# Gathered token columns packed to 104 a pass instead of 128, in a two-layer decoder step with routed experts

## The reference

```python
scores = jax.nn.sigmoid(x @ router_w)                  # 320 tokens x 64 experts
_, eidx = lax.top_k(jnp.where(emask, sel, -jnp.inf), 8)  # 8 experts a token
w = take(scores, eidx); w = w / sum(w) * 2.5
# for each expert e, over the tokens that chose it:
hb = jax.nn.silu(xb @ wg[e]) * (xb @ wu[e])            # 1024 -> 256
y[tok] += (hb @ wd[e]) * w[:, None]                    # 256 -> 1024
```

## Time and profile before

| | |
|---|---|
| median of 3 runs | 1434.81 us (1434.44 to 1436.46) |
| the profiled execution | 1434.92 us, its span in the trace 1433.1 us |
| TensorE (PE) busy | 1395.9 us, 97% |
| VectorE (DVE) busy | 437.7 us, 31% |
| ScalarE (ACT) busy | 317.1 us, 22% |
| expert loop of layer 0 | 247.5 to 705.7 us |
| expert loop of layer 1 | 954.5 to 1412.6 us |
| loads by SyncE's queue | 489.96 MB of 509.52 MB |

### The profile page before, as it was taken

How to read it: one execution, slowest core, us unless ns; L and a number is a source line. 1 busy time by engine, 2 the same in 40 slices (tenths; PEclk the granted TensorE clock), 3 DMA queues, 4 the chain that set the end, 5 groups by cost and what they waited for, 6 DMA issues and landing times.

```text
span 1433.1 us, 20787 instructions
## 1 busy us (share of the span) xinstructions
PE 1395.9 (97%) x8288; PEld 706.4 (49%) x8288; DVE 437.7 (31%) x1161; ACT 317.1 (22%) x746; POOL 48.1 (3%) x86
## 2 busy tenths in 40 slices
PE   7999999999999999999999999999999999999997
PEld 3345657444445444444465456564444444444443
DVE  1146535312221222122345243442121312122214
ACT  2134323111111111111345113411111111111113
POOL 0100302000000000000100010010000000000000
PEclk9999999999999999999999999999999999999998
DMA  9999528999999999999972245389999999999993
GB/s 393 389 381 427 214 103 311 392 390 427 421 423 426 421 425 425 424 426 424 422 320 118 118 162 219 112 336 380 425 424 423 426 423 421 425 424 426 425 424 126
DMA packets 48002, 509.52 MB, mean 356 GB/s; under 512 B 5808, under 2 KB 6208, under 8 KB 8320
## 3 DMA queue, kind: packets, MB, share of 16 engines
q1 hardware_dynamic: 44144, 489.96, 82.1%
q0 software_dynamic: 3760, 18.20, 3.4%
HBM read 499.10 MB, written 11.01 MB: 356 GB/s over the span
## 4 chain that ended last, share of the span: by engine, by line
PE 88%; DMA 4%; DVE 3%; ACT 3%; issue 1%; SPq 0%; DVEq 0%; ACTq 0%
PE bank L2044 26%; PE banks L2094 13%; PE banks L1946 10%; PE banks L442 5%; PE ybank L1974 3%; PE banks L1119 3%; PE banks L1974 3%; PE bank L1976 3%; DMA s_gu_ring<-in_moe_up_dram 3%; PE bank L504 2%; PE ybank L1738 1%; PE banks L1738 1%; DMA s_gu_ring<-in_ada_w_dram 1%; PE banks L697 1%; PE banks L1124 1%; PE banks L671 1%
## 5 line engine op out<-in xcount | busy, mean ns | idle before, releaser
L2044 PE MATMUL bank<-s_gu_ring,s_hbuf 128*32 128x512 f32 (+1 forms) x2688 | 395.2, 593 | 1.4 <-DVE s_hbuf L2169 0.9
L2044 PEld LDWEIGHTS bank<-s_gu_ring,s_hbuf 128*32 128x32 f32 (+1 forms) x2688 | 121.9, 119 | 265.9 <-issue 265.9
L2094 PE MATMUL banks<-s_dn_ring,s_hTs 128*32 128x512 f32 (+1 forms) x1344 | 204.2, 596 | 0.0
L2214 DVE TENSOR_TENSOR s_ylo<-banks,s_yhi 128x512 fp32r<-128x512 f32 x112 | 77.5, 692 | 320.2 <-ACT s_yhi L2136 320.2
L1946 PE MATMUL banks<-s_sel,s_htok 128*128 128x512 f32 (+1 forms) x640 | 144.8, 374 | 0.5 <-issue 0.5
L1946 PEld LDWEIGHTS banks<-s_sel,s_htok 128*128 128x128 f32 x640 | 106.2, 188 | 60.7 <-issue 44.3
L2136 ACT CAST s_yhi<-banks 128x512 fp32r<-128x512 f32 x112 | 65.7, 586 | 296.5 <-PE banks L2094 296.5
L2209 DVE SCALAR_TENSOR_TENSOR s_hh<-s_sg,s_wsl,bank 128x256 f32<-128x256 f32 x56 | 26.9, 480 | 288.1 <-ACT s_sg L2127 288.1
L2094 PEld LDWEIGHTS banks<-s_dn_ring,s_hTs 128*32 128x32 f32 (+1 forms) x1344 | 55.9, 118 | 118.0 <-issue 117.3
L2127 ACT ACTIVATE s_sg<-bank 128x256 f32<-128x256 f32 x56 | 21.6, 385 | 364.8 <-PE bank L2044 364.8
L2169 DVE COPY s_hbuf<-banks 128x512 f32<-128x512 f32 (+1 forms) x60 | 39.4, 656 | 96.0 <-PE banks L1946 96.0
(11 more groups left out here) (463 smaller groups left out, 1452.5 us busy)
## 6 DMA issues: line engine op xcount, KB each, us to landing
s_gu_ring<-in_moe_up_dram SPq DMA_DIRECT2D x128, 2048.0 KB, 15.2
s_dn_ring<-in_moe_wd_dram SPq DMA_DIRECT2D x128, 1024.0 KB, 12.8
s_gu_ring<-in_ada_w_dram SPq DMA_DIRECT2D x24, 2048.0 KB, 13.0
s_gu_ring<-in_win_dram SPq DMA_DIRECT2D x6, 2048.0 KB, 12.8
s_gu_ring<-in_wqkv_dram SPq DMA_DIRECT2D x6, 1024.0 KB, 19.4
s_gu_ring<-in_wo_dram SPq DMA_DIRECT2D x2, 2048.0 KB, 18.8
s_gu_ring<-in_shared_up_dram SPq DMA_DIRECT2D x2, 2048.0 KB, 9.8
s_gu_ring<-in_gwo_dram SPq DMA_DIRECT2D x2, 2048.0 KB, 10.8
```

What stands on the lines that cost most here:

```text
L2044: last = pe.matmul(W0[o:o + n, :], tokens_of(p, k)[:, o:o + n], w[:, k, :, :], start=(k == 0), stop=(k == KC - 1))
L2094: last = pe.matmul((W1, W2)[half][o:o + n, :], hTs[:, f, o:o + n], dn_ring[:, DN_PLACE[dn_of[(l, r)][0]], w0:w0 + 512], start=(f == 0), st ...
L2214: dve.tensor_tensor(ylo[:, half, :], (W1, W2)[half], yhi[:, half, :].bitcast(F32), ALU.subtract).then_inc(S["y_low"], 1)
```

## The change

Each rank gets a number of gathered columns of its own (`ROOMS`, at most its capacity), and a pass has `PITCH[q]` gathered columns: 104, and 112 in batch 1. `gathered` gives each rank's first column. The rows of the pass, its capacities and the weight loads' sizes stay as they are. So:

- `select` writes one instruction for each rank, with as many columns as its room; fills move 416 columns (448 in batch 1, 208 in batches 0 and 7).
- The gate and up products still take 32, 64 or 96 rows for a rank, from its packed first column on; beyond its room they read the next rank's tokens.
- `spread` takes the place of `dense`: it clears `selb` and copies each rank's columns to its row places, so rows beyond a room have weight zero.
- At the start of a layer's loop VectorE clears columns 104 to 127 of every block of `hbuf`, after it has waited for fill 1.
- `pass_plan` pairs the fullest ranks with the emptiest: (2, 63), (3, 62) and so on, and among the 64-row ranks the first with the last.
- `sg` and `hTs` move into the router's memory, and `selb` gets its own.

```diff
+ROOMS = (
+    (52, 52, 96, 93, 92, 85, 82, 82, 80, 76, 63, 62, 60, 60, 58, 57, 56, 55, 54, 54, 52, 52,
...
+PITCH = (104, 112, 104, 104, 104, 104, 104, 104)
...
-    wide = [[(NFIX + i, 96), (NE - n96 + i, 32)] for i in range(n96)]
-    middle = [[(r, 64), (r + 1, 64)] for r in range(first64, first32 - light, 2)]
+    wide = [[(NFIX + i, 96), (NE - 1 - i, 32)] for i in range(n96)]
+    middle = [[(first64 + i, 64), (last64 - 1 - i, 64)] for i in range((last64 - first64) // 2)]
...
+def gathered(l, experts):
+    out, at = [], 0
+    for r, cap, o in places(experts):
+        out.append((r, ROOMS[l][r], o, at))
+        at += ROOMS[l][r]
+    return out
...
-                        width = P * BATCHES[q]
+                        width = PITCH[q] * BATCHES[q]
...
-                                last = pe.matmul(W0[o:o + n, :], tokens_of(p, k)[:, o:o + n], w[:, k, :, :],
+                                last = pe.matmul(W0[o:o + n, :], tokens_of(p, k)[:, o - back_by[r]:o - back_by[r] + n], w[:, k, :, :],
...
+                        w = PITCH[q]
                         for h in range(BATCHES[q]):
+                            for r, n, _, at in gathered(l, PASSES[l][BATCH_START[q] + h]):
+                                last = dve.tensor_tensor(sel[:, :, h * w + at:h * w + at + n],
...
-                    def dense(q):
-                        n = P * BATCHES[q]
-                        for t, (t0, tn) in enumerate(TILES):
-                            last = dve.tensor_copy(selb[t][0:tn, 0:n], sel[0:tn, t, 0:n].bitcast(F32))
+                    def spread(q):
+                        step(dve.memset(selb[:, :, 0:P * BATCHES[q]], 0.0))
+                        w = PITCH[q]
+                        for h in range(BATCHES[q]):
+                            for r, n, o, at in gathered(l, PASSES[l][BATCH_START[q] + h]):
+                                last = dve.tensor_copy(selb[:, :, h * P + o:h * P + o + n], sel[:, :, h * w + at:h * w + at + n].bitcast(F32))
...
+                    dve.wait_ge(S["fill_full"], filled(0, 1))
+                    dve.memset(hbuf[:, :].rearrange("p (x s) -> p x s", s=P)[:, :, PITCH[0]:P], 0.0)
                     fill_out(0, 1)
                     fill_out(0, 3)
```

More of the change, by code:

```diff
@@ L151, in const_table @@
     put("keyrow", np.broadcast_to(NE - 1 - np.arange(NE) + ahead, (P, NE)))
-    for name, plan in zip(("caprow", "caprow1"), PASSES):
-        cap = np.zeros(NE)
-        for r, slots in sum(plan, []):
-            cap[r] = slots
-        put(name, np.broadcast_to(cap, (P, NE)))
+    for name, room in zip(("caprow", "caprow1"), ROOMS):
+        put(name, np.broadcast_to(np.array(room), (P, NE)))
     half = HD // 2
@@ L1955, in slot_weights @@
                             for s, (t0, tn) in enumerate(TILES):
-                                last = pe.matmul(W0[:, at:at + n6].rearrange("p (e u) -> p e u", u=6), selb[s][0:tn, P * j:P * j + P],
+                                last = pe.matmul(W0[:, at:at + n6].rearrange("p (e u) -> p e u", u=6), selb[0:tn, s, P * j:P * j + P],
                                                  wpartS[0:tn, s, :, ranks[0]:ranks[-1] + 1:ranks[1] - ranks[0]].rearrange("p u e -> p e u"), start=(s == 0), stop=(s == 2))
@@ L2179, in _ @@
                     dve.wait_ge(S["sel_full"], l * NB + 1)
-                    dense(0).then_inc(S["w_parts"], 1)
+                    spread(0).then_inc(S["w_parts"], 1)
                     dve.wait_ge(S["sh_silu"], 2 * l + 2)
@@ L2199, in _ @@
                     step(select(1))
-                    dense(1).then_inc(S["sel_full"], 1)
+                    spread(1).then_inc(S["sel_full"], 1)
                     dve.wait_ge(S["wall_full"], l * NB + 1)
@@ L2222, in _ @@
                             step(select(q + 2))
-                            dense(q + 2).then_inc(S["sel_full"], 1)
+                            spread(q + 2).then_inc(S["sel_full"], 1)
                     rest_dve(dve, left)
```

49 lines of the change are left out of this document (21 added, 28 removed), and 5 rows, old and new, of the table ROOMS.

## The result

The changed kernel takes 1438.45 us (median of 12 runs, 1437.48 to 1441.66), the kernel before in the same series 1435.16 us (12 runs, 1434.44 to 1436.67). The ratio is 1.0021, with a 95% interval of 1.0014 to 1.0029: slower by 3.3 us by the medians and by 3.0 us by the ratio. The prediction set 0.2% as the bound between "within" and "slower", and the interval reaches to both sides of it. The forecast was 1435.3 us with a range of 1430.5 to 1439.5, and "within 0.2%" had the most of the three chances (0.57; slower had 0.20). The profiled execution took 1437.77 us (before 1434.92), its span is 1436.0 us (before 1433.1).

A forecast was written before the change was run, and what follows sets the result against it. The prediction took the load queue as the bound, 0.35 us longer than TensorE's chain. From 1434.92 us it took 3.4 for earlier loads and added 3.8 for the low clock: 1435.3 us, range 1430.5 to 1439.5.

The forecast's parts named there:

- What bounds the kernel: Expert loops: the load queue outlasts TensorE's work by 0.35 us, so TensorE's saved 11.2 us a layer mostly becomes load waits.
- The rival with TensorE as the bound: Whole run: the queue can exceed 426 GB/s, so all 22.4 us saved on TensorE arrive; 1412.5 us, chance 0.03.
- The clock: Pass 27 of each layer: the wait ahead drops TensorE to half rate, losing 1.9 us a layer, 3.8 us in both.
- a start that it called a hint: Kernel start: matmuls reached full pace after 4.3 us, about 3.7 us of it work; gave the 1.9 us loss.
- the clock holds: Rival, last passes: the clock stays full through the waits, so only the queue's gain counts; 1431.5 us, chance 0.18.
- The long low clock: Rival, pass 27: half rate through all gate and up products costs 7.1 us a layer; 1445.7 us, chance 0.08.
- The start of the loop: First pass of a layer: starts 0.2 us earlier, with bounds from 0.6 us earlier to 0.6 us later.
- The load queue: Each layer's last load lands 1.7 us earlier, 1.3 us from the loads behind pass 2; 3.4 us in both layers.
- small gaps: Later loop slices at 420 to 424 GB/s instead of 426: closing them gives the load queue 0.4 us a layer.
- `spread` and `hh`: `spread` ends about 253.3, 1 us before needed: no wait; `hh` may show 0.1 to 0.2 us in four passes.
- VectorE's chain at the start: Rival: first pass starts 0.6 us late and is held up 0.8 us, cancelling the queue's gain; 1438.7 us, chance 0.12.
- The change does what it says: Rival: a rank exceeds its room, so `rest` reloads 64 experts, 201 MB or 473 us; 1908 us, chance 0.01.

The follow-up runs named there:

- light kernels: Kernel before and changed kernel, each loading only half of every expert's down weights, used twice: 4250.14 and 4231.72 us; only layer 0's loop is comparable.
- awake2: Changed kernel plus 11 and 22 extra small matmuls on TensorE ahead of the load waits of passes 26 and 27: 1434.95 us, ratio 1.0000.
- pool: Changed kernel with the clearing of `hbuf`'s columns moved from VectorE to GpSimd: 1439.32 us, ratio 1.0026 to the kernel before.
- hold_awake: awake2 with each layer's last three down loads issued only once its last gate/up load has landed: 1440.49 us, ratio 1.0041.
- hold_best: Changed kernel, shared down products moved as in shift_after, 7 and 22 extra matmuls, last three down loads held as in hold_awake: 1434.00 us, ratio 0.9990.
- shift_after: Changed kernel with the shared expert's down products for tokens 0 to 127 moved from pass 1's end to behind pass 2's gate/up products: 1436.15 us.
- wide: Changed kernel with rooms equal to capacities and pitch 128 again, nothing cleared in `hbuf`, new pairing and `spread` kept: 1435.19 us, ratio 1.0000.
- light_before: Kernel before, loading only the first half of each expert's down weights and using it twice, which changes layer 1's routing: 4250.14 us.

## Why the prediction was right in kind, and what it mis-sized

**What bounds the kernel.** Right. TensorE's saving became waits for loads at the places and of the lengths forecast (5.80 for 5.9 us; 3.06 for some 3 us), and the light kernels show that the saving is real (9.9 us a layer from pass 0 on; the prediction's 11.2 contained 1.7 us for 208 columns, and its own caveat was more than half right: 1.21 for 1.29 us a ten, 0.7 us in all). The rival with TensorE as the bound is out.

**The clock.** Right that it falls and costs time at pass 27, and near in size. In layer 0 it fell in the wait as forecast; in layer 1 only 0.8 us after the wait had ended. It cost 8.40 - 7.07 = 1.33 us in layer 0 and 8.77 - 7.07 = 1.70 us in layer 1. Together 3.0 us in the profile and 3.0 to 3.5 us in the runs (awake2 against the changed kernel), for which the prediction had 3.8. What was left of the low clock when layer 0's load had landed was 2.7 us (691.32 to 694.05), and half of that is the 1.33 us lost. In layer 1 all of it lay in the pass (1400.61 to 1404.02). The forecast took its price from a start that it called a hint, so that it is this near is in part luck. The rival "the clock holds" is out by awake2. The long low clock, through all the gate and up products, is out by the stretch 694 to 696, at 0.99, in the first half of pass 27. The Trainium skill, "TensorE: Matmul & The Clock Gate", section "What's actually happening", has idle time bring the low clock back. The fall at 690 to 692 agrees; the one at 1400.61 came when TensorE was at work again. Pass 26 of layer 0, at 7.07 us after a wait of 3.06, shows that a wait of that length doesn't always do it.

**The start of the loop.** Mis-sized. Forecast: 0.2 us earlier. Measured: pass 0 starts 6.29 us behind the first fill for 5.93, 0.36 us later in both layers. The step that failed is the fill of 208 columns. Ten were to take 1.08 us; the first 30 took 3.57, 1.19 a ten. The first fill also began 0.08 us later. The second fill had ended at 243.95 instead of 243.7, and VectorE's memset began at 244.41 instead of 243.9, so some 0.2 us of its delay came between the two and has no cause shown; the memset itself (0.70 us) was as forecast. The measured value was inside the bounds of -0.6 to +0.6 that were given. pool moves this term and the time does not follow, so it matters only through the next one.

**The load queue.** This is the term that failed: 1.7 us a layer forecast, 3.4 us in both. In the profile pass 27 starts 0.56 us earlier in layer 0 and 0.34 us *later* in layer 1. In the runs awake2, which has the narrow columns and no low clock, stands at 1.0000 of the kernel before, with an interval of 1.3 us to both sides. Its first step was right: from pass 0 to the loads behind pass 2 are 292.94 - 247.95 = 44.99 us instead of 46.10, which is the 1.1 us of two passes' fills. With the later start 0.75 us remain in layer 0 (0.65 in layer 1), where 1.3 was forecast: 1.2 us of the missing 3.2 us for both layers. The 0.4 us a layer of small gaps came as forecast: from 100 to 446.4 us behind the first fill the queue moved 0.2 MB more than before, 0.5 us.

What failed besides is the step from the whole queue to one load, "so the last load of a layer lands 1.7 us earlier". I added up the queue's packets in the traces, from the issue of a layer's first expert load, 55.6 us ahead of its first fill. At 446.4 us behind the first fill the changed kernel had moved 195.10 MB in layer 0 and 195.06 in layer 1, the kernel before 194.62 in both: at 425 GB/s the queue was 1.1 and 1.0 us ahead. But when the last gate and up load landed, 196.38 and 196.66 MB had moved, before only 196.16 and 196.08. In hold_awake and hold_best, where nothing stands behind that load, it is 195.04 MB. So 1.0 to 1.1 MB of later loads had moved in the kernel before by the time the slowest DMA engine ended its part of the last one, and in the changed kernel 0.2 and 0.6 MB more, which is 0.5 and 1.4 us. That leaves 1.1 - 0.5 = 0.6 us earlier and 1.0 - 1.4 = 0.4 us later, which is what pass 27 did (0.56 and 0.34). Why the engines lay further apart in the changed kernel stays open; landings scatter by 1 us between single profiles, so it may be chance. That the size of the hole matters at all is shown by shift_after: closing some 2 us of idle queue a layer (the queue was 0.80 and 0.84 MB further at 446.4 us than in the changed kernel) moved pass 27 by 1.9 us in both layers, and the time by 2.3 us.

**Sum.** With the measured terms: 1434.92 + 3.0 (clock) - 0.2 (pass 27, -0.56 + 0.34) + 0.1 (first fill at 241.66 for 241.58) = 1437.8 us, and the profiled execution took 1437.77. The forecast of 1435.3 missed that by 2.5 us: the queue term promised 3.2 us too much, the clock's term took 0.8 us too much, and 0.1 us is the later first fill. That the clock's error hid a part of the queue's is luck. The median lies another 0.7 us above the profiled execution.

**`spread` and `hh`.** Right: no wait. `selb` was done at 253.2 (forecast 253.3) and wide shows that the pairing and `spread` are free. The rival "VectorE's chain at the start" has nearly the right time (1438.7) for a wrong reason: nothing held up pass 0 there, and taking the clearing off VectorE (pool) did not bring the time down.

**The change does what it says.** No leftover path ran in the changed kernel. light_before shows that the price put on it, 473 us for 201 MB at 426 GB/s, was far too low: with the path taken in layer 1 it took 4250.14 us, some 2800 us more than the kernel before. From 2000 to 3000 us its loads moved at 70 GB/s, so the queue's full rate was the wrong bound for that rival.

## What to carry to other kernels

Where two chains are of nearly equal length, shortening one of them buys a wait, and a wait on TensorE is not free: here 9.9 us of saved work a layer came back in layer 0 as 8.9 us of waits (3.06 and 5.80) and 1.3 us lost at half rate. Before narrowing work on an engine, lighten the other chain in an experiment to see what the saving is worth alone, then look for the stretches in which the bounding queue is idle: 2 us of hole closed in each layer gave 2.3 us in all, 10 us of TensorE work a layer gave none. If a wait ahead of the last pass can't be avoided, cheap matmuls into a free bank in its place bring back the clock's loss, provided that they are sized by a measured duration. And a queue that is ahead by so many bytes does not land its last load that much earlier: here the load waited for the slowest of the DMA engines.

## What the runs showed of the hardware

- A filler matmul of 128 columns in float32 shows as two instructions and takes 0.23 us, start to start (96 instructions in 10.9 us).
- The pace of the fills is not linear in columns below 256: ten take 1.21 us at 208 columns, 1.29 at 256, 2.00 at 416 and 2.41 at 512. From 256 to 416 that is 0.44 ns a column and matmul, from 416 to 512 0.43, from 208 to 256 only 0.17. The row for 208, start to start:

```profile
615.23 1.37 PE L1962 MATMUL banks<-s_sel,s_htok 128*128 128x208 f32 x10
616.44 0.44 PE L2087 MATMUL bank<-s_cst,s_hh 128*128 128x128 f32 x2
```

- The clock also fell away from the loops in some executions. In the profile of shift_after it read 0.50 between the layers, on work that is the same in all kernels, and in that of pool too; in that of the changed kernel it did not:

```profile
874.00:876.00 2.00, 1.95 (x7) 1.78 (x8) 0.00 (x0) 0.09 (x1) 0.89 (x1) 0.50 0.04 14
```

- A load issued 9 us earlier into a full queue landed 0.5 us earlier; its time from issue to landing says where the queue stands, not how fast a load is.
- The same wait of 3.0 us ahead of pass 26 left the clock at full rate in layer 0 and lowered it in layer 1. Ahead of pass 27 in layer 1 the wait of 4.17 us passed at full rate, and the clock fell 0.8 us after work had begun again.
- The DMA engines do not end their parts of a load together: in hold_awake the share of busy engines fell from 0.81 to 0.48 to 0.08 over the last 8 us before the last gate and up load was in.
